# Attention denominators from three bf16 pieces, and outputs turned six slots after a block's end

## The reference, cut to what matters

```python
def block(args):
    qn, qr = args
    s = (jnp.einsum('bqhd,bkhd->bhqk', qn, k_nope)
         + jnp.einsum('bqhd,bkd->bhqk', qr, k_rope)).astype(jnp.float32) * scale
    p = jax.nn.softmax(s, axis=-1).astype(v.dtype)
    return jnp.einsum('bhqk,bkhd->bqhd', p, v)
```

## Time and profile before

| | us |
|---|---|
| median of 3 runs | 3552.84 (3548.39 to 3555.3) |
| the profiled execution | 3554.7 |
| its span, first to last instruction | 3552.9 |
| PE busy | 3386.2 (95%) |
| DVE busy | 2219.0 (62%) |
| ACT busy | 1570.1 (44%) |
| POOL busy | 836.3 (24%) |

### The profile page before, as it was taken

The page is one execution under the profiler, slowest core; times in us unless marked ns, Lnnn a source line. Parts: engine busy times, 40 slices in busy tenths (PEclk is TensorE's granted clock), DMA queues, the critical chain, the costliest instruction groups (busy, mean ns, idle before and its releaser), DMA issues. The chain is left out here.

```text
span 3552.9 us, 51356 instructions
## 1 busy us (share of the span) xinstructions
PE 3386.2 (95%) x18881; PEld 2930.6 (82%) x18882; DVE 2219.0 (62%) x3907; ACT 1570.1 (44%) x2019; POOL 836.3 (24%) x417
## 2 busy tenths in 40 slices
PE   7999979997999999999899669999999999999996
PEld 6888868885777777777688569999999999999995
DVE  5444447766888888887555565555555555555578
ACT  2111124444777777777333313333333333333476
POOL 0000000004777777777111101111111111111111
PEclk9999989998999999999899779999999999999998
DMA  4333356767223322210333325555555555555675
GB/s 150 112 112 112 112 184 236 265 238 203 42 61 72 70 59 48 49 40 13 122 142 142 125 90 169 171 171 171 171 171 171 171 171 171 171 171 171 207 264 205
DMA packets 348064, 506.10 MB, mean 142 GB/s; under 512 B 106288, under 2 KB 242224, under 8 KB 342688
## 3 DMA queue, kind: packets, MB, share of 16 engines
q1 hardware_dynamic: 334848, 457.38, 39.3%
q0 software_dynamic: 13088, 47.06, 5.6%
HBM read 366.02 MB, written 138.36 MB: 142 GB/s over the span
## 5 line engine op out<-in xcount | busy, mean ns | idle before, releaser
L63 PE MATMUL psum<-xeT_hi,w_hi 128*128 128x320 f32 x2048 | 634.4, 310 | 0.0
L65 PE MATMUL psum<-xeT_hi,w_lo 128*128 128x320 f32 x2048 | 632.8, 309 | 0.0
L64 PE MATMUL psum<-xeT_lo,w_hi 128*128 128x320 f32 x2048 | 632.8, 309 | 0.0
L2379 DVE TENSOR_TENSOR w_lo<-shared,w_hi 128x2048 fp32r<-128x2048 f32 x190 | 427.5, 2284 | 32.3 <-ACT w_hi L2214 32.2
L2214 ACT ACTIVATE w_hi<-shared 128x2048 fp32r<-128x2048 f32 x192 | 358.2, 1907 | 187.2 <-PE psum L65 187.2
L63 PEld LDWEIGHTS psum<-xeT_hi,w_hi 128*128 128x128 f32 x2048 | 384.4, 188 | 0.9
L64 PEld LDWEIGHTS psum<-xeT_lo,w_hi 128*128 128x128 f32 x2048 | 384.5, 188 | 0.6
L65 PEld LDWEIGHTS psum<-xeT_hi,w_lo 128*128 128x128 f32 x2048 | 384.5, 188 | 0.0
L1438 DVE TENSOR_REDUCE mx<-psum 128x1 f32<-128x1024 f32 x256 | 312.0, 1222 | 22.8 <-PE psum L1288 21.5
L2027 POOL DMA_INDIRECT xe<-x,idx_next x48 | 76.8, 1600 | 932.3 <-DVE gate_next L2411 865.8
L1374 ACT ACTIVATE psum<-psum 128x1024 f32<-128x1024 f32 x272 | 274.2, 1008 | 8.6
(11 more groups left out here) (401 smaller groups left out, 7513.8 us busy)
## 6 DMA issues: line engine op xcount, KB each, us to landing
shared<-in_w_gate SPq DMA_DIRECT2D x64, 1024.0 KB, 5.6
shared<-in_w_up SPq DMA_DIRECT2D x64, 1024.0 KB, 7.1
shared<-in_w_down SPq DMA_DIRECT2D x64, 1024.0 KB, 5.1
xT<-xaT SPq DMA_DIRECT2D x20, 1024.0 KB, 6.4
rec<-rec SPq DMA_DIRECT2D x20, 768.0 KB, 3.6
shared<-rec SPq DMA_DIRECT2D x20, 768.0 KB, 5.3
shared<-in_x SPq DMA_DIRECT2D x20, 512.0 KB, 4.8
cq_hi<-xT SPq DMA_DIRECT2D x20, 512.0 KB, 6.3
```

The costliest lines, as they stand in the source:

```text
L63: pe.matmul(out, a[0], b[0], start=first, stop=False)
L64: pe.matmul(out, a[0], b[1], start=False, stop=False)
L65: return pe.matmul(out, a[1], b[0], start=False, stop=last)
L2379: v.tensor_tensor(w_lo[n % 4][:], raw[n % 4], w_hi[n % 4][:].bitcast(F32), ALU.subtract).then_inc(s["lo_made"], 1)
```

## The change

Three things are done to every block but the last two (`WHOLE` is 38).

The denominators' four fp32 matmuls become twelve bf16 ones. The tile `added_up` is split into three bf16 pieces whose sum is the fp32 tile: ScalarE copies it to bf16 (`take_first`), GpSimd subtracts that from the tile in place (`take_rest`), ScalarE copies the remainder to bf16 (`take_second`), GpSimd subtracts again and writes the third piece (`take_third`). Each query group of 128 is then multiplied piece by piece with a bf16 column of ones, three matmuls into one PSUM column.

The turn moves from loop last+2 to last+6 (last+7 for the prompt's fourth block and for the two-slot block of a head). `take_out` stays in loop last+1; since the tiles are read later, `o_a`, `o_b` and the pieces have two sets each. The last two blocks are turned in loop last+2 as before.

The value tiles `v_lo_hi` shrink from 192 to 130 columns a key tile, with a gap tile behind each; what is read and written of them is the same.

```diff
-        VW = 3 * MV
-        vals = [sb(f"v_lo_hi{b}", [P, NT, VW], F32R) for b in range(2)]
+        VW = 2 * MV + 2
+        vals = [(sb(f"v_lo_hi{b}", [P, NT, VW], F32R), sb(f"gap_v{b}", [P, 24]))[0] for b in range(2)]
...
-        turn_slot = {g + 2: n for n, g in enumerate(last_of)}
-        out_slot = {g + 3: n for n, g in enumerate(last_of)}
-        turn_at = [g + 2 for g in last_of]
+        WHOLE = NBH - 2
+        turn_at = [g + (2 if n >= WHOLE else 6 if n % NB < 3 else 7) for n, g in enumerate(last_of)]
+        turn_slot = {g: n for n, g in enumerate(turn_at)}
+        out_slot = {g + 1: n for n, g in enumerate(turn_at)}
+        first_slot = {g + 2: n for n, g in enumerate(last_of) if n < WHOLE}
+        second_slot = {g + (4 if n % NB < 3 else 5): n for n, g in enumerate(last_of) if n < WHOLE}
...
+                    if n < WHOLE:
+                        pe.wait_ge(s["third_made"], n + 1)
+                        pe.wait_ge(s["ones_set"], 1)
+                    else:
+                        pe.wait_ge(s["p_added_up"], n + 1)
                     for q in range(4):
                         at = 4 * (MV + 1) + 2 * q
-                        ins = pe.matmul(ps[:, 6, at:at + 1], added_up[n % 2][:, q * P:(q + 1) * P], ones[:, 0:1],
-                                        start=True, stop=True)
+                        if n < WHOLE:
+                            for k in range(3):
+                                ins = pe.matmul(ps[:, 6, at:at + 1], pieces[n % 2][k][:, q * P:(q + 1) * P], ones_bf[:, 0:1],
+                                                start=k == 0, stop=k == 2)
...
+                def take_first(n):
+
+                    a.wait_ge(s["p_added_up"], n + 1)
+                    wait_from_one(a, s["out_turned"], n - 1)
+                    a.activation(pieces[n % 2][0][:], added_up[n % 2][:], ACT.Copy).then_inc(s["first_made"], 1)
+
+                def take_second(n):
+
+                    a.wait_ge(s["rest_made"], n + 1)
+                    a.activation(pieces[n % 2][1][:], added_up[n % 2][:], ACT.Copy).then_inc(s["second_made"], 1)
...
+                def take_rest(n):
+
+                    g.wait_ge(s["first_made"], n + 1)
+                    g.tensor_tensor(added_up[n % 2][:], added_up[n % 2][:], pieces[n % 2][0][:], ALU.subtract
+                                    ).then_inc(s["rest_made"], 1)
+
+                def take_third(n):
+
+                    g.wait_ge(s["second_made"], n + 1)
+                    wait_from_one(g, s["out_turned"], n - 1)
+                    g.tensor_tensor(pieces[n % 2][2][:], added_up[n % 2][:], pieces[n % 2][1][:], ALU.subtract
+                                    ).then_inc(s["third_made"], 1)
+
+                rests, thirds = {}, {}
+                for n in range(WHOLE):
+                    done = adds_before[n + 1]
+                    rests.setdefault(done + 2, []).append(n)
+                    thirds.setdefault(done + (5 if n % NB == 4 else 4), []).append(n)
```

More of the change, by code:

```diff
@@ L1144, in attention_phase @@
                       for a, n in enumerate(("hi", "lo")))
-        o_a, o_b = sb("o_a", [P, 512]), sb("o_b", [MV + 1, 512])
+        pieces = [[sb(f"added_piece{k}{b}", [P, 512], BF16) for k in range(3)] for b in range(2)]
+        ones_bf = sb("ones_bf", [P, 2], BF16)
+        o_a = [sb(f"o_a{b}", [P, 512]) for b in range(2)]
+        o_b = [sb(f"o_b{b}", [MV + 1, 512]) for b in range(2)]
         small = sb("small_part", [P, 4])
@@ L1157, in attention_phase @@
         names = ("constant_rows scored hi_made raw_made lo_made mixed unit_scored unit_reduced mx4_made "
-                 "o_taken out_turned half_taken small_taken sums_made den_made half_added o_summed o_made p_added p_added_up").split()
+                 "o_taken out_turned half_taken small_taken sums_made den_made half_added o_summed o_made p_added p_added_up "
+                 "first_made rest_made second_made third_made ones_set").split()
         s = {n: c.sem("m_" + n) for n in names}
@@ L1337, in turn_out @@
                     pe.wait_ge(s["o_taken"], n + 1)
-                    pe.wait_ge(s["p_added_up"], n + 1)
                     wait_from_one(pe, s["o_summed"], n)
                     for q in range(4):
-                        pe.transpose(ps[:, 5, q * P:(q + 1) * P], o_a[:, q * P:(q + 1) * P], c.ident)
+                        pe.transpose(ps[:, 5, q * P:(q + 1) * P], o_a[n % 2][:, q * P:(q + 1) * P], c.ident)
                     for q in range(4):
-                        pe.transpose(ps[:, 6, q * (MV + 1):(q + 1) * (MV + 1)], o_b[:, q * P:(q + 1) * P],
+                        pe.transpose(ps[:, 6, q * (MV + 1):(q + 1) * (MV + 1)], o_b[n % 2][:, q * P:(q + 1) * P],
                                      c.const[0:MV + 1, C_ID:C_ID + MV + 1])
+                    if n < WHOLE:
[3 more added lines that the diff above has]
+                        pe.wait_ge(s["p_added_up"], n + 1)
                     for q in range(4):
                         at = 4 * (MV + 1) + 2 * q
-                        ins = pe.matmul(ps[:, 6, at:at + 1], added_up[n % 2][:, q * P:(q + 1) * P], ones[:, 0:1],
-                                        start=True, stop=True)
+                        if n < WHOLE:
+                            for k in range(3):
+                                ins = pe.matmul(ps[:, 6, at:at + 1], pieces[n % 2][k][:, q * P:(q + 1) * P], ones_bf[:, 0:1],
+                                                start=k == 0, stop=k == 2)
+                        else:
+                            ins = pe.matmul(ps[:, 6, at:at + 1], added_up[n % 2][:, q * P:(q + 1) * P], ones[:, 0:1],
+                                            start=True, stop=True)
                     ins.then_inc(s["out_turned"], 1)
@@ L1377, in take_out @@
                     a.wait_ge(s["mixed"], last_of[n] + 1)
-                    wait_from_one(a, s["out_turned"], n)
-                    a.activation(o_b[:], ps[0:MV + 1, 7, :], ACT.Copy)
-                    a.activation(o_a[:], ps[:, 4, :], ACT.Copy).then_inc(s["o_taken"], 1)
+                    wait_from_one(a, s["out_turned"], n - 1)
+                    a.activation(o_b[n % 2][:], ps[0:MV + 1, 7, :], ACT.Copy)
+                    a.activation(o_a[n % 2][:], ps[:, 4, :], ACT.Copy).then_inc(s["o_taken"], 1)
+                def take_first(n):
+                    a.wait_ge(s["p_added_up"], n + 1)
+                    wait_from_one(a, s["out_turned"], n - 1)
+                    a.activation(pieces[n % 2][0][:], added_up[n % 2][:], ACT.Copy).then_inc(s["first_made"], 1)
+                def take_second(n):
+                    a.wait_ge(s["rest_made"], n + 1)
+                    a.activation(pieces[n % 2][1][:], added_up[n % 2][:], ACT.Copy).then_inc(s["second_made"], 1)
                 def take_half(n):
@@ L1391, in _ @@
                         take_out(last_of.index(g - 1))
+                    if g in first_slot:
+                        take_first(first_slot[g])
+                    if g in second_slot:
+                        take_second(second_slot[g])
                     if g in turn_slot:
@@ L1407, in _ @@
                     g.memset(part.bitcast(F32), value).then_inc(s["constant_rows"], 1)
+                g.memset(ones_bf[:], 1.0).then_inc(s["ones_set"], 1)
+                def take_rest(n):
[12 more added lines that the diff above has]
+                    thirds.setdefault(done + (5 if n % NB == 4 else 4), []).append(n)
                 adds = 0
@@ L1421, in _ @@
                         adds += 1
+                        for n in rests.get(adds, ()):
+                            take_rest(n)
+                        for n in thirds.get(adds, ()):
+                            take_third(n)
                     g.wait_ge(s["p_added"], adds)
-                    wait_from_one(g, s["out_turned"], k - 1)
+                    if k < WHOLE:
+                        wait_from_one(g, s["third_made"], k - 1)
+                    else:
+                        g.wait_ge(s["third_made"], k - 1)
                     g.tensor_tensor(added_up[k % 2][:], acc[:, 0, :], acc[:, 1, :], ALU.add).then_inc(s["p_added_up"], 1)
```

## The result

The changed kernel takes 3528.03 us (median of 4 runs, 3526.19 to 3530.38), the kernel before, run beside it, 3553.26 (4 runs): ratio 0.993, with a 95% interval of 0.9919 to 0.9941. The forecast was 3544 us in a range of 3530 to 3562. A gain of 25 us stands where 9 were forecast. The mean granted clock of single runs lies between 0.970 and 0.975, and the 27 runs of the kernel before in the first batch of experiments spread over 9 us with it (3556.15 us at 0.972, 3547.06 at 0.974), so 2 us between two medians say little.

The account below looks back on a forecast made before the run. The prediction took TensorE's row of work as the bound (busy 823 of 833 us in attention). Cheaper sums of -19.8 us and held multiplies of +11.2 gave -8.6, hence 3544 us on the median's scale, range 3530 to 3562.

Parts of the forecast that it names:

- bf16 sums: TensorE's turn slot: twelve bf16 matmuls take 0.35 us instead of 0.87 for four fp32, 38 times: -19.8 us.
- held multiply, fourth block: Fourth block's turn: line 1476's multiply waits for GpSimd's add, row maxima 1.2 us late: 1.1 us, 7 heads.
- held multiply, two-slot block: Two-slot block's turn: multiply wanted at 28.4, add ends at 28.6, a fold follows; between 0 and 1.3, taken 0.5 us.
- line-1451 copy and the turn beside it: Loop last+4: score 0.1 us late instead of 0.69, but second block's turn waits 0.5 us for row maxima; together nothing.
- narrow value tiles: Mix's weight loads: narrower value tiles change only the stride, 0.19 us behind a matmul of 0.23; taken as nothing.
- ScalarE's copies: Two copies a block fit into 0.73 us idle before exponentials: nothing; 7.6 us if 0.1 us stuck out of each.
- block 36: Its turn moves to where no units are left: 0 to 1.9 us of gain, taken as none.
- rival 4: Turn's bf16 passes cost the fp32 price: 3581 us; chance 0.05 together with a turn waiting for its third piece.
- rival 3: Ordinary blocks: GpSimd chain 0.3 us slower pushes each of 24 turns about 0.3, ScalarE's copies stick out: 3554 us; chance 0.14.
- GpSimd's steps: GpSimd stepped through: adds 2.39 us, subtractions 1.29, gaps 0.08; fourth block's add ends at 21.94, multiply wanted at 20.36.
- rival 1: Turn's multiply is not held by GpSimd, 0.42 us throughout: 3533 us, or 3531 with block 36; chance 0.27.
- Rival 2: GpSimd starts its next instruction before waiting VectorE gets in: multiply waits 6 us more, copy another 2.4: 3605 us; chance 0.09.

Follow-up runs that it names:

- last experiment: Changed kernel with the 4-column copy as a reduction and the two-slot block's turn in last+8 instead of last+7: 3521.39 us, ratio 0.991.
- the two reduction experiments: Kernel before with line 1451's copy as a reduction: 3546.59 us; changed kernel with line 1534's multiply as a one-input reduction, division left out: 3523.07 us.

## Why the prediction missed

The terms as they were put, and as they came out (a head is 34 slots, five turns):

| term | forecast | measured |
|---|---|---|
| bf16 sums | -0.52 x 38 = -19.8 | -0.54 x 38 = -20.5 |
| held multiply, fourth block | +1.1 x 7 | 0 |
| held multiply, two-slot block | +0.5 x 7 | +0.55 x 7 = +3.9 |
| line-1451 copy and the turn beside it | 0 | -0.72 x 8 = -5.8 |
| narrow value tiles | 0 | -0.23 x 8 = -1.8 |
| ScalarE's copies; the slot of `take_out` | 0 | +0.17 x 7 = +1.2 |
| block 36 | 0 | about 0 |
| two slots of 3.10 and 3.12 us, ordinary with the change | 0 | -0.66 |
| sum | -8.6 | -23.7 |

The two slots are the third of the fourth head and the nineteenth of the sixth. They take 3.08 to 3.12 us in all five profiles that turn in loop last+2, and are ordinary in the four with the moved turn; why stays open. From the first mix to the last, and without the last slot, the profiles differ by 24.6 us, the medians by 25.2; so 1 to 1.5 us are not assigned. The value tiles' -1.8 in slots is -4.6 in time, and the interval (0 to -6.4) holds both.

**The sums** were right: twelve bf16 passes cost about what rows 4 said (0.31 us for 0.35; rival 4 wanted 1.31). Nor did rival 3 come about: ordinary turn slots are 3.41 us, so no chain on GpSimd pushed them.

**GpSimd's steps failed**: the table of starts and ends that the prediction worked out for GpSimd, and with it the fourth block's 7.7 of the 15.1 us between the two sums. The subtractions were taken at the fold's 1.29 us, and the space in front of every instruction as the fold's 0.08. A subtraction takes 1.17 us, and the spaces differ: in the records an add and a subtraction next to each other overlap by 0.04 to 0.05 us, in either order, a fold starts 0.08 behind what is in front of it, and an add starts 0.14 behind an add (the row of 4.95 us is two adds of 2.40 and that space). To the place where the fourth block's multiply is wanted the steps hold eight instructions, three of them subtractions, and seven spaces: 16.38 us, from 5.56 to 21.94. The trace has 15.39 (1058.47 to 1073.87). Of the 1.0 us between them the subtractions are 0.36 and the spaces 0.70; the adds, 0.01 us longer each, take 0.07 back. The multiply comes 0.37 us late there, not 1.6, and that much is hidden: the slot behind the turn takes 3.52 us with the multiply and 3.52 with the reduction that isn't held. A bf16 operand was in sight in rows 10; at 0.899 us for 320 columns it said nothing of what 512 columns gain over fp32.

**The two-slot block's 0.5 us came true by luck.** It was a choice between 0 and 1.3, for a multiply that meets the last 0.2 us of an add (28.4 and 28.6) with a fold behind it. In the trace the add is over (1080.08) when the multiply is wanted (1080.37), the fold has run for 0.2 us, and the multiply is held for 0.93 us, of which 0.55 stick out. Two errors, GpSimd's steps too long and a turn put 1.1 us too late by the fourth block's delay, moved both ends.

**The copy of line 1451 was under-credited**, by the same steps. "Together nothing" priced the copy's stall going from 0.69 to 0.1 against a turn that waits 0.5 us in loop last+6. The stall went (the copy takes 0.67 us, forecast about 1.2). The wait did not come. The steps let the third piece end 1.13 us after the copy is wanted (12.90 less 11.77); it ends 0.64 after (1017.86 less 1017.22). By these numbers the forecast's wait of 0.5 us is that half microsecond (an estimate: no run puts it back): with it gone the lo tile and the row maxima are in time, and the turn there costs 0.07 us more than another. With the copy not held at all even that goes (3.40 us, last experiment), and with the copy behind an add it is 1.2 us (5.18 against 3.97, the moved turn alone). So the failed step accounts for some 13 of the 15.1 us.

**The hold itself** was predicted rightly, against rival 1: the multiply takes 0.42 us in pauses, 0.79 and 1.36 under GpSimd (longest 1357 ns), and only 0.42 when it is a reduction with one input (mean of all 40). The Trainium skill, page "SBUF — State Buffer", section "Who interferes with whom", has the same rule, and adds that a `tensor_reduce` never contends on trn2; the two reduction experiments (0.16 and 0.42 us under a running GpSimd instruction) agree. Whoever reads the rule should price the place at which it strikes: of the 15 multiplies that were held, the seven under a fold are the ones that cost TensorE time.

**Rival 2 is refuted.** VectorE's instruction gets in between two GpSimd instructions that follow without a pause, and none of the 23 held ones (15 multiplies, 8 copies) waits for a second: the CAST ends at 1017.89, the subtraction in front of it at 1017.86, and the add behind it is on record from 1017.82. At the boundary the multiply ends at 1074.15, 0.28 us behind the two adds, while the third piece is already on record from 1073.83.

**ScalarE's copies** were put at nothing. TensorE never waits for the pieces, but in loop last+1 of the two-slot block a slot takes 3.07 us against 2.89 in the other blocks. In the experiment with the moved turn and no copies to bf16 it takes 3.06 as well: so it belongs to the moved turn, and the new copies cost nothing that shows. The steps had no term for it.

## What to carry to other kernels

A held instruction costs only what it sticks out of the slack at its place, and a change of order moves holds that already exist: list those too, since here one that went away was worth 5.8 us. When an engine is stepped through, each instruction needs its own duration and its own pause; 0.12 us in each of eight makes 1 us at the end, which is more than the slack that was being decided. Where a copy, or an instruction with both inputs in SBUF, meets GpSimd's work on VectorE, try a reduction that gives the same numbers (where there is one, as for the small copy), or a loop in which GpSimd pauses, before moving anything larger.

## What was not expected of the hardware

- GpSimd subtracts a bf16 tile from an fp32 tile of 128x512 in 1.17 us; the fp32 fold of the same size takes 1.29.
- GpSimd's pauses depend on the pair: 0.14 us between two adds to the same tile, 0.08 before a fold, and none between an add and a subtraction.
- GpSimd's instruction is stretched while VectorE's two-input instruction runs at its start: 1.35 us instead of 1.17 for line 1452, in which the 0.28 us of the multiply's end lie. With the multiply as a reduction it takes 1.16 at the same place (1073.51 above).
- Ordinary slots take 2.77 instead of 2.79 us when the value tile's key tiles stand 520 instead of 768 bytes apart. Only the weight loads of the mix read that tile. No run shows which step of TensorE it is.
